# Cross attention block of a hybrid decoder step: order of the first loads and scores

## The chip, the cores and the metric

The kernel runs on 1 core of one Trainium2 chip. The metric is the device time of one execution in microseconds, as the median of several runs. The engines are called PE (TensorE), DVE (VectorE), ACT (ScalarE), POOL (GpSimd) and SP (SyncE, which issues DMAs).

## The reference, cut to what matters

The reference is one inference step of two trunk layers over two groups, a prompt of 1024 rows and a sample group of 8 sequences with 4 rows each. Each layer has a mixer and then a gated cross attention into 256 memory tokens with 4 heads of width 256. The prompt attends to keys and values made in the step, each sample sequence to its own cached keys and values:

```python
def cross_attn(h, mk, mv, w_qg, w_o):
    b, t, _ = h.shape
    q, g = jnp.split(h @ w_qg, 2, axis=-1)
    q = q.reshape(b, t, X_HEADS, X_HEAD_DIM)
    s = jnp.einsum('bthd,bmhd->bhtm', q, mk).astype(F32) * (X_HEAD_DIM ** -0.5)
    p = jax.nn.softmax(s, axis=-1).astype(h.dtype)
    o = jnp.einsum('bhtm,bmhd->bthd', p, mv).reshape(b, t, D_MODEL)
    return (o * jax.nn.silu(g)) @ w_o
```

## The kernel before, in words

In each of the two layers `cross_attention` (L2376) makes the prompt's keys KM and values VM, projects queries QT and gates SGX, runs `cross_both` (L2124), and then the output projection. Each of these parts is a block of its own: its instructions start when the block before is left, except that an engine with nothing more to do there is early and waits. The change is in `cross_both` alone.

`cross_both` has eight rounds and a ninth to drain. Round i works on tile i of the prompt (128 rows) and on sample sequence i. For the prompt, `scores` (L2184) makes the scores of a head in PSUM tile xS, `maximum` (L2275) reduces all four heads, `exponent` (L2338) exponentiates a head, `normalise` (L2281, L2283) scales, `turn` (L2197) and `turned` (L2348) transpose the probabilities, `values` (L2208) and `outputs` (L2289) make the result. For the sample, the cached keys of a sequence (1 MB, 128 partitions with two memory rows of 4 KB each) are loaded into one of two slots KB (L2156); `sample_keys` (L2220) turns a quarter of them, which is one head, with four transposes into the one PSUM tile zT; `sample_keys_out` (L2293) copies it to SBUF, and the next quarter may be turned only then. `sample_scores` (L2231) wants all four quarters. `sample_maximum` (L2299), `sample_exponent` (L2356) and `sample_normalise` (L2305, L2306) follow; the last multiplies with a column of the owner table xown, which is 1 where a row of the 32 belongs to the sequence. `sample_turn` (L2238), `sample_turned` (L2362) and `sample_values` (L2246) end the sequence, the last with the cached values (1 MB, two slots VB, L2175).

The order of work on each engine is written out by hand, engines meet by semaphores. A score call of one head shows as four matmul instructions in the trace, and four transposes make a quarter. In every round TensorE does `scores` and `sample_keys` of one head after the other, four times, then `turn` of the tile before, `sample_scores`, `values` and `sample_values` of the round before, `sample_turn`. VectorE does the four copies, then `maximum` and `sample_maximum`. SyncE asks for the keys of sequences 0 and 1 at once, then for the owner table (L2158) and for the gain vector gb of the output norm (L2159, read by the output projection), and for the keys of a later sequence once the slot's keys are turned (semaphore z_tp); after them come the output weights WO (L2163, L2166). GpSimd asks for the values of sequences 0 and 1 at once, and for later ones once the slot's value product is done (z_pv). VectorE waits for the owner table (z_m) before its first instruction in the block.

Of the kernel before, what the change touches and what calls it, by code (L numbers as in the profile page):

```python
# [22 lines left out]
P = 128  # L23
# [3 lines left out]
NB, TS = 8, 4  # L27
SMP = NB * TS
TOK = TP + SMP
NQ = TP // P  # L30
# [11 lines left out]
XH, XD = 4, 256  # L42
# [86 lines left out]
def build(nc, A, O):  # L129
# [4 lines left out]
    def sem(name):  # L134
        return top.enter_context(nc.semaphore(name))
# [1825 lines left out]
    def memory_keys_values(l, KM, VM, rows=(), gain=None, HT=None):  # L1961
# [153 lines left out]

    x_sc, x_nm, x_ex, x_pn, x_tp, x_te, x_pv, x_oe = (sem(n) for n in (
        "x_scores", "x_negmax", "x_exp", "x_normed", "x_probs_tp", "x_probs_out", "x_pv", "x_pv_out"))
    z_l, z_lv = [sem(f"memk_slot{k}") for k in range(2)], [sem(f"memv_slot{k}") for k in range(2)]
    z_m, z_tp, z_te, z_sc, z_nm, z_ex, z_pn, z_pt, z_pe, z_pv, z_oe = (sem(n) for n in (
        "z_mask", "z_k_tp", "z_k_out", "z_scores", "z_negmax", "z_exp", "z_normed", "z_probs_tp", "z_probs_out", "z_pv",  # L2120
# [3 lines left out]
    def cross_both(l, room, KM, VM, QT, SGX, WO, gb):  # L2124
# [5 lines left out]
        n0 = NQ * l  # L2130
        with ExitStack() as c:
# [17 lines left out]
            @block.sync  # L2149
            def _(sp):  # L2150
                w = A["x_w_o"][l].rearrange("(k p) n -> p k n", p=P)
                for b in range(NB):
                    if b >= 2:

                        sp.wait_ge(z_tp, 4 * (n0 + b - 1))
                    sp.dma_start(KB[b % 2], ck[:, b]).then_inc(z_l[b % 2], 16)  # L2156
                    if b == 1:
                        sp.dma_start(own[:], A["c_batch4"]).then_inc(z_m, 16)  # L2158
                        sp.dma_start(gb[:], A["norm_post_x"][l].partition_broadcast(P)).then_inc(y_g, 16)  # L2159

                for a in range(2):
                    sp.wait_ge(z_tp, 4 * (n0 + NB - 1 + a))
                    sp.dma_start(WO[:, 2 * a:2 * a + 2, :], w[:, 2 * a:2 * a + 2, :]).then_inc(y_w, 16)  # L2163
                for a in range(2):
                    sp.wait_ge(z_pv, n0 + NB - 1 + a)
                    sp.dma_start(WO[:, 4 + 2 * a:6 + 2 * a, :], w[:, 4 + 2 * a:6 + 2 * a, :]).then_inc(y_w2, 16)  # L2166
                sp.wait_ge(v_vout, 16 * (l + 1))

            @block.gpsimd
            def _(pool):  # L2170
                for b in range(NB):
                    if b >= 2:

                        pool.wait_ge(z_pv, n0 + b - 1)
                    pool.dma_start(VB[b % 2], cv[:, b]).then_inc(z_lv[b % 2], 16)  # L2175

            @block.tensor
            def _(pe):
                def scores(i, h):
                    if h == 0 and i:  # L2180

                        pe.wait_ge(x_ex, n0 + i)
                    for k in range(2):
                        m = nc.tensor.matmul(S[:, h * MEM:(h + 1) * MEM], QT[:, 2 * h + k, i * P:(i + 1) * P],  # L2184
                                             KM[:, 2 * h + k, :], start=k == 0, stop=k == 1)
                    if h == XH - 1:
                        m.then_inc(x_sc, 1)

                def turn(i):
                    pe.wait_ge(x_pn, n0 + i + 1)  # L2190
                    for a in range(2):
                        if i:

                            pe.wait_ge(x_te, 2 * (n0 + i - 1) + a + 1)
                        for h in (2 * a, 2 * a + 1):
                            for k in range(2):
                                t = nc.tensor.transpose(TPp[a][:, (2 * (h % 2) + k) * P:(2 * (h % 2) + k + 1) * P],  # L2197
                                                        PB[i % 2][:, h, k * P:(k + 1) * P], ident[:])
                        t.then_inc(x_tp, 1)

                def values(i, a):
                    pe.wait_ge(x_te, 2 * (n0 + i) + a + 1)
                    if 2 * i + a:

                        pe.wait_ge(x_oe, 2 * (n0 + i) + a)
                    for d in range(4 * a, 4 * a + 4):
                        for k in range(2):
                            m = nc.tensor.matmul(OV[:, d % 4 * P:(d % 4 + 1) * P], VM[:, k, d * P:(d + 1) * P],  # L2208
                                                 PT[i % 2][:, d // 2 * 2 + k, :], start=k == 0, stop=k == 1)
                    m.then_inc(x_pv, 1)  # L2210

                def sample_keys(b, q):
                    if q == 0:
                        pe.wait_ge(z_l[b % 2], 16 * (NB // 2 * l + b // 2 + 1))
                    if 4 * b + q:

                        pe.wait_ge(z_te, 4 * (n0 + b) + q)
                    for k in range(2):
                        for n in range(2):
                            t = nc.tensor.transpose(KTp[:, (2 * k + n) * P:(2 * k + n + 1) * P],  # L2220
                                                    KB[b % 2][:, n, (2 * q + k) * P:(2 * q + k + 1) * P], ident[:])
                    t.then_inc(z_tp, 1)

                def sample_scores(b):
                    pe.wait_ge(z_te, 4 * (n0 + b + 1))
                    if b:

                        pe.wait_ge(z_pe, n0 + b)
                    for k in range(2):
                        for h in range(XH):  # L2230
                            m = nc.tensor.matmul(SS[32 * h:32 * h + 32, 0:MEM], QT[:, 2 * h + k, TP:TOK], KBT[b % 2][:, 2 * h + k, :],  # L2231
                                                 start=k == 0, stop=k == 1, tile_position=(0, 32 * h))
                    m.then_inc(z_sc, 1)

                def sample_turn(b):
                    pe.wait_ge(z_pn, n0 + b + 1)
                    for k in range(2):
                        t = nc.tensor.transpose(SS[:, MEM + k * P:MEM + (k + 1) * P], PZ[b % 2][:, k * P:(k + 1) * P], ident[:])  # L2238
                    t.then_inc(z_pt, 1)

                def sample_values(b):
                    pe.wait_ge(z_pe, n0 + b + 1)
                    pe.wait_ge(z_lv[b % 2], 16 * (NB // 2 * l + b // 2 + 1))
                    for k in range(2):
                        for h in range(XH):
                            m = nc.tensor.matmul(OS[32 * h:32 * h + 32, 0:XD], PZT[b % 2][:, k, 32 * h:32 * h + 32],  # L2246
                                                 VB[b % 2][:, k, h * XD:(h + 1) * XD], start=b == 0 and k == 0,
                                                 stop=b == NB - 1 and k == 1, tile_position=(0, 32 * h), skip_group_check=True)
                    m.then_inc(z_pv, 1)

                for i in range(NQ + 1):
                    for h in range(XH):
                        if i < NQ:
                            scores(i, h)
                            sample_keys(i, h)
                    if i:
                        turn(i - 1)
                    if i < NQ:
                        sample_scores(i)
                    if i:  # L2260
                        values(i - 1, 0)
                        sample_values(i - 1)
                        values(i - 1, 1)
                    if i < NQ:
                        sample_turn(i)
                pe.wait_ge(z_oe, 3 * l + 1)
                for k in range(2):
                    t = nc.tensor.transpose(SS[:, k * P:(k + 1) * P], OZ[:, k * P:(k + 1) * P], ident[:])
                t.then_inc(z_pt, 1)

            @block.vector
            def _(dve):
                def maximum(i):
                    dve.wait_ge(x_sc, n0 + i + 1)
                    nc.vector.tensor_reduce(nm[:, i % 2, :], S[:].rearrange("p (h m) -> p h m", h=XH), AX.X, ALU.max, negate=True)\  # L2275
                        .then_inc(x_nm, 1)
# [28 lines left out]
                    dve_own.step(dve, nc.vector.reciprocal(zi[:, v], zsum[:, v]))  # L2305
                    nc.vector.tensor_scalar(PZ[b % 2][:], PZ[b % 2][:], zi[:, v], own[:, b:b + 1], ALU.mult, ALU.mult).then_inc(z_pn, 1)  # L2306

                dve.wait_ge(z_m, 16 * (l + 1))
                for i in range(NQ + 1):
                    if i < NQ:  # L2310
                        for q in range(4):
                            sample_keys_out(i, q)
                        maximum(i)
                        sample_maximum(i)
                    if i:
                        outputs(i - 1, 0)
                    if i < NQ:
                        sample_normalise(i)
                        normalise(i)
                    if i:  # L2320
                        outputs(i - 1, 1)
# [1020 lines left out]
```

## Time and profile before

| | us |
|---|---|
| median of 3 runs | 3042.34 |
| lowest and highest run | 3032.16, 3043.95 |
| the profiled execution, whole | 3035.24 |
| its span in the profile | 3033.5 |
| TensorE busy in it | 2711.2 |

The span runs from the first to the last instruction of the profiled execution; the execution's own time is 1.7 us longer. In the timeline a row gives the start, the duration, the engine, the line of the kernel and the names; a number in brackets is the idle time of that engine before the row, and what ended it. WO is the tile in which the slots KB and VB lie, HT the one with the turned keys and probabilities.

### The profile page before, as it was taken

Reading aid. Unit: us, or ns where it says so; the run is one execution under the profiler, and the core shown is the slowest. Engines: PE = TensorE matmul, PEld = TensorE weight load, DVE = VectorE, ACT = ScalarE, POOL = GpSimd, SP = SyncE. Lnnn points to the kernel's source line nnn. Section 1 sums busy time; section 2 is a strip of 40 time slices with the busy share of each in tenths; the row PEclk is TensorE's granted clock in tenths of the full one; section 3 lists DMA queues with packets and bytes.
Section 4 is the critical chain, followed back from the end, with each engine's and each line's share of the span. In section 5 each row is a group of like instructions: output and inputs, shape, how many; then the busy total and the mean of one; then the engine's idle time right before and its main releaser. Section 6 shows DMA issues by size and latency. Waiting matters only on the chain. (4 is left out here: it accounts for less than half of the span.)

```text
span 3033.5 us, 40100 instructions
## 1 busy us (share of the span) xinstructions
PE 2711.2 (89%) x16263; PEld 2170.5 (72%) x16263; DVE 1453.6 (48%) x2550; ACT 777.8 (26%) x1466; POOL 520.9 (17%) x419
## 2 busy tenths in 40 slices
PE   5999899998978998997999689776999996899898
PEld 4999566676766996686999467654555555699677
DVE  4998666564421004534665431156777673200453
ACT  3221355232312212322322112122121212221231
POOL 1012000341311210131212000012212221121012
PEclk9999899997989998997999799897998998999999
DMA  3211010862032114302322222284423203211531
GB/s 99 65 35 48 21 36 18 304 238 88 1 95 85 43 42 160 125 1 54 99 84 77 90 70 74 75 302 127 125 62 106 81 16 111 83 43 42 175 119 49
DMA packets 237754, 270.75 MB, mean 89 GB/s; under 512 B 36566, under 2 KB 190742, under 8 KB 232355
## 3 DMA queue, kind: packets, MB, share of 16 engines
q1 hardware_dynamic: 217762, 179.85, 20.0%
q0 software_dynamic: 16384, 75.77, 6.9%
q10 hardware_dynamic: 3456, 12.98, 1.0%
q8 instruction: 112, 1.84, 0.3%
q14 instruction: 40, 0.33, 0.0%
HBM read 226.66 MB, written 41.28 MB: 88 GB/s over the span
## 5 line engine op out<-in xcount | busy, mean ns | idle before, releaser
L297 PE MATMUL pp<-HH,WS_part 128*128 128x352 f32 x1776 | 574.2, 323 | 0.0
L295 PE MATMUL pp<-HH,WH 128*128 128x352 f32 x1344 | 436.3, 325 | 34.9 <-POOL WS_part L434 34.9
L296 PE MATMUL pp<-HT_part,WH 128*128 128x352 f32 x1344 | 434.5, 323 | 0.0
L297 PEld LDWEIGHTS pp<-HH,WS_part 128*128 128x128 f32 x1776 | 336.7, 190 | 0.0
L295 PEld LDWEIGHTS pp<-HH,WH 128*128 128x128 f32 x1344 | 254.2, 189 | 38.1 <-POOL WS_part L434 38.1
L296 PEld LDWEIGHTS pp<-HT_part,WH 128*128 128x128 f32 x1344 | 254.4, 189 | 0.0
L2293 DVE COPY HT<-zT 128x512 f32<-128x512 f32 x64 | 44.3, 692 | 437.0 <-DMA xown<-c_batch 383.8
L434 POOL TENSOR_TENSOR WS_part<-WS,WH 128x1024 fp32r<-128x1024 f32 x56 | 142.6, 2547 | 603.2 <-ACT WH L385 603.2
L2873 PE MATMUL OP<-oWO,YT 128*128 128x512 f32 x512 | 223.0, 593 | 1.3 <-DVE XE L3014 0.6
L2873 PEld LDWEIGHTS OP<-oWO,YT 128*128 128x128 f32 x512 | 96.5, 190 | 120.6 <-issue 119.8
L1048 DVE SCALAR_TENSOR_TENSOR CV<-GXP,cw,CV 128x512 f32<-128x512 f32 x240 | 161.9, 740 | 0.0
L295 PE MATMUL pp<-HH,CK_part 128*128 128x352 f32 x432 | 141.9, 328 | 7.9 <-DVE HT_part L913 7.9
L296 PE MATMUL pp<-HT_part,CK_part 128*128 128x352 f32 x432 | 140.4, 325 | 0.0
L295 PE MATMUL zp<-WZH,HH 128*128 128x512 f32 x256 | 103.9, 406 | 15.6 <-ACT ZS L2705 11.0
L2853 POOL TENSOR_TENSOR XK<-XK,Db 128x2048 f32<-128x2048 f32 (+1 forms) x9 | 88.1, 9788 | 141.9 <-DVE XD L3040 141.9
L295 PE MATMUL yp<-QT_part,KM_part 128*128 128x512 f32 x256 | 102.2, 399 | 2.3 <-DVE WO_part L628 2.3
L2509 DVE SCALAR_TENSOR_TENSOR oACC<-EP,cwo,oACC 128x1024 f32<-128x1024 f32 x72 | 98.7, 1370 | 9.2 <-DVE oACC L2507 2.4
L297 PE MATMUL zp<-WZH,HT_part 128*128 128x512 f32 x256 | 102.4, 400 | 0.0
L296 PE MATMUL zp<-WZ_part,HH 128*128 128x512 f32 x256 | 102.2, 399 | 0.0
L297 PE MATMUL yp<-QT_part,SGX_part 128*128 128x512 f32 x256 | 101.9, 398 | 0.0
L296 PE MATMUL yp<-WO_part,KM_part 128*128 128x512 f32 x256 | 101.7, 397 | 0.0
L2917 PEld LDWEIGHTS U<-XD,CBt 128*128 128x128 f32 (+1 forms) x576 | 78.6, 220 | 21.2 <-issue 16.4
(519 smaller groups left out, 5172.8 us busy)
## 6 DMA issues: line engine op xcount, KB each, us to landing
WS<-x_w_qg SPq DMA_DIRECT2D x32, 512.0 KB, 4.1
WO<-cache_mem_k SPq DMA_DIRECT2D x16, 1024.0 KB, 5.0
WO<-cache_mem_v POOLq DMA_DIRECT2D x16, 1024.0 KB, 5.6
CBt<-cum_scratch SPq DMA_DIRECT2D x8, 2048.0 KB
xbc_scratch<-oACC ACTq DMA_DIRECT2D x24, 528.0 KB, 2.7
WS<-o_w_in SPq DMA_DIRECT2D x24, 512.0 KB, 3.9
XT<-xbc_scratch SPq DMA_DIRECT2D x8, 1536.0 KB, 7.8
WS<-e_w_in SPq DMA_DIRECT2D x18, 512.0 KB, 3.9
```

Of the source, the lines that this page charges most:

```text
L295: nc.tensor.matmul(out, wh, xh, start=start, stop=False)
L296: nc.tensor.matmul(out, wh, xl, start=False, stop=False)
L297: return nc.tensor.matmul(out, wl, xh, start=False, stop=stop)
L434: nc.gpsimd.tensor_tensor(WL[:, k % slots, :, :], WS[:, k % slots, :, :], WH[k % 2][:, :, :], ALU.subtract).then_inc(p_lo, 1)
L1048: ins = nc.vector.scalar_tensor_tensor(out=out, in0=src, scalar=tap, in1=out, op0=ALU.mult, op1=ALU.add)
L2293: nc.vector.tensor_copy(KBT[b % 2][:, 2 * q:2 * q + 2, :], KTp[:].rearrange("p (k m) -> p k m", k=2))\
L2509: ins = nc.vector.scalar_tensor_tensor(out=out, in0=src, scalar=tap, in1=out, op0=ALU.mult, op1=ALU.add)
L2853: nc.gpsimd.tensor_tensor(XK[R, :].rearrange("p (h e) -> p h e", h=SH), XK[R, :].rearrange("p (h e) -> p h e", h=SH), Db[R, :].unsqueeze(2 ...
L2873: m = nc.tensor.matmul(OP[hf][0:T, :], YT[:, k, 0:T], WO[:, k, hf * 512:(hf + 1) * 512], start=k == 0, stop=k == NX - 1)
L2917: m = nc.tensor.matmul(U[g % 2][R, e * SP_:(e + 1) * SP_], CB[R, h, R], XD[R, h * SP_:(h + 1) * SP_], start=True, stop=True)
```

## The change

The first sequence's keys are requested in four column quarters, each with a semaphore z_q of its own, and each quarter's turning waits for its own semaphore. The owner table is requested directly behind the quarters, the keys of sequence 1 behind it, and gb behind the last key request. In round 0 TensorE makes the scores of all four heads of tile 0 before it turns a key; VectorE takes their maximum first, then copies, and waits for the owner table just before the first sample maximum. GpSimd requests the values of sequence 0 when two quarters of its keys are turned, those of sequence 1 when all four are. The waits on the two key slots are counted anew, since sequence 0 no longer signals them. Nothing in the arithmetic changes.

```diff
--- before.py
+++ after.py
@@ -2115,6 +2115,7 @@
 
     x_sc, x_nm, x_ex, x_pn, x_tp, x_te, x_pv, x_oe = (sem(n) for n in (
         "x_scores", "x_negmax", "x_exp", "x_normed", "x_probs_tp", "x_probs_out", "x_pv", "x_pv_out"))
+    z_q = [sem(f"memk_first{q}") for q in range(4)]
     z_l, z_lv = [sem(f"memk_slot{k}") for k in range(2)], [sem(f"memv_slot{k}") for k in range(2)]
     z_m, z_tp, z_te, z_sc, z_nm, z_ex, z_pn, z_pt, z_pe, z_pv, z_oe = (sem(n) for n in (
         "z_mask", "z_k_tp", "z_k_out", "z_scores", "z_negmax", "z_exp", "z_normed", "z_probs_tp", "z_probs_out", "z_pv",
@@ -2149,14 +2150,16 @@
             @block.sync
             def _(sp):
                 w = A["x_w_o"][l].rearrange("(k p) n -> p k n", p=P)
-                for b in range(NB):
+                for q in range(4):
+                    cols = slice(2 * q * P, (2 * q + 2) * P)
+                    sp.dma_start(KB[0][:, :, cols], ck[:, 0, :, cols]).then_inc(z_q[q], 16)
+                sp.dma_start(own[:], A["c_batch4"]).then_inc(z_m, 16)
+                for b in range(1, NB):
                     if b >= 2:
 
                         sp.wait_ge(z_tp, 4 * (n0 + b - 1))
                     sp.dma_start(KB[b % 2], ck[:, b]).then_inc(z_l[b % 2], 16)
-                    if b == 1:
-                        sp.dma_start(own[:], A["c_batch4"]).then_inc(z_m, 16)
-                        sp.dma_start(gb[:], A["norm_post_x"][l].partition_broadcast(P)).then_inc(y_g, 16)
+                sp.dma_start(gb[:], A["norm_post_x"][l].partition_broadcast(P)).then_inc(y_g, 16)
 
                 for a in range(2):
                     sp.wait_ge(z_tp, 4 * (n0 + NB - 1 + a))
@@ -2169,8 +2172,9 @@
             @block.gpsimd
             def _(pool):
                 for b in range(NB):
-                    if b >= 2:
-
+                    if b < 2:
+                        pool.wait_ge(z_tp, 4 * n0 + 2 * b + 2)
+                    else:
                         pool.wait_ge(z_pv, n0 + b - 1)
                     pool.dma_start(VB[b % 2], cv[:, b]).then_inc(z_lv[b % 2], 16)
 
@@ -2210,8 +2214,12 @@
                     m.then_inc(x_pv, 1)
 
                 def sample_keys(b, q):
-                    if q == 0:
-                        pe.wait_ge(z_l[b % 2], 16 * (NB // 2 * l + b // 2 + 1))
+                    if b == 0:
+                        pe.wait_ge(z_q[q], 16 * (l + 1))
+                    elif q == 0 and b % 2 == 0:
+                        pe.wait_ge(z_l[0], 16 * ((NB // 2 - 1) * l + b // 2))
+                    elif q == 0:
+                        pe.wait_ge(z_l[1], 16 * (NB // 2 * l + b // 2 + 1))
                     if 4 * b + q:
 
                         pe.wait_ge(z_te, 4 * (n0 + b) + q)
@@ -2249,9 +2257,13 @@
                     m.then_inc(z_pv, 1)
 
                 for i in range(NQ + 1):
+                    if i == 0:
+                        for h in range(XH):
+                            scores(0, h)
                     for h in range(XH):
+                        if 0 < i < NQ:
+                            scores(i, h)
                         if i < NQ:
-                            scores(i, h)
                             sample_keys(i, h)
                     if i:
                         turn(i - 1)
@@ -2305,12 +2317,15 @@
                     dve_own.step(dve, nc.vector.reciprocal(zi[:, v], zsum[:, v]))
                     nc.vector.tensor_scalar(PZ[b % 2][:], PZ[b % 2][:], zi[:, v], own[:, b:b + 1], ALU.mult, ALU.mult).then_inc(z_pn, 1)
 
-                dve.wait_ge(z_m, 16 * (l + 1))
+                maximum(0)
                 for i in range(NQ + 1):
                     if i < NQ:
                         for q in range(4):
                             sample_keys_out(i, q)
-                        maximum(i)
+                        if i:
+                            maximum(i)
+                        else:
+                            dve.wait_ge(z_m, 16 * (l + 1))
                         sample_maximum(i)
                     if i:
                         outputs(i - 1, 0)
```

## Rows read from the trace of the kernel before

**Rows 1.** The page: span and busy time of each engine (us, share, instructions).

```profile
span 3033.5 us, 40100 instructions
PE 2711.2 (89%) x16263; PEld 2170.5 (72%) x16263; DVE 1453.6 (48%) x2550; ACT 777.8 (26%) x1466; POOL 520.9 (17%) x419
```

**Rows 2.** Source line 2293: what its engine waited for (us, times), both layers.

```profile
  DMA xown<-c_batch: 383.8, 2
```

**Rows 3.** Timeline, layer 0: start, duration, engine, line, names [idle before, releaser].

```profile
1143.53 0.88 SPq L2156 DMA_DIRECT2D WO<-cache_mem_k  x2
...
1143.58 1.10 PE L2184 MATMUL xS<-KM,QT 128*128 128x256 f32 x4 [0.81 <-PEq L2392]
...
1150.28 1.12 PE L2220 MATMUL zT<-ident,WO 128*128 128x128 f32 x4 [5.59 <-DMA WO<-cache_mem_k]
...
1156.73 0.69 DVE L2293 COPY HT<-zT 128x512 f32<-128x512 f32 x1 [193.43 <-DMA xown<-c_batch]
...
1158.63 0.69 DVE L2293 COPY HT<-zT 128x512 f32<-128x512 f32 x1 [1.21 <-PE zT L2220]
...
1164.20 1.07 PE L2231 MATMUL zS<-HT,QT 128*32 128x256 f32 x16 [0.78 <-DVE HT L2293]
...
1166.23 0.47 ACT L2356 ACTIVATE PZ<-zS,znm 128x256 f32<-128x256 f32 x1
...
1167.49 0.69 PE L2238 MATMUL zS<-ident,PZ 128*128 128x128 f32 x2 [2.22 <-DVE PZ L2306]
...
1181.37 0.72 POOL L2175 DMA_DIRECT2D WO<-cache_mem_v  x1 [35.79 <-PE zO L2246]
1194.05 0.71 POOL L2175 DMA_DIRECT2D WO<-cache_mem_v  x1 [11.96 <-PE zO L2246]
```

**Rows 4.** Timeline, layer 1, the same events.

```profile
2809.65 1.10 PE L2184 MATMUL xS<-KM,QT 128*128 128x256 f32 x4 [0.81 <-PEq L2392]
...
2814.75 0.89 PE L2220 MATMUL zT<-ident,WO 128*128 128x128 f32 x4 [3.99 <-DMA WO<-cache_mem_k]
...
2827.13 1.07 PE L2231 MATMUL zS<-HT,QT 128*32 128x256 f32 x16 [0.78 <-DVE HT L2293]
...
2830.42 0.44 PE L2238 MATMUL zS<-ident,PZ 128*128 128x128 f32 x2 [2.22 <-DVE PZ L2306]
...
2841.76 0.71 POOL L2175 DMA_DIRECT2D WO<-cache_mem_v  x1 [29.82 <-PE zO L2246]
```

**Rows 5.** Timeline, layer 1: maximum of the scores, then a key step of sequence 1.

```profile
2826.99 1.22 DVE L2275 TENSOR_REDUCE xnm<-xS 128x4 f32<-128x1024 f32 x1
...
2833.03 0.66 PE L2220 MATMUL zT<-ident,WO 128*128 128x128 f32 x4
...
2833.53 1.03 PE L2184 MATMUL xS<-KM,QT 128*128 128x256 f32 x4
2833.73 0.69 DVE L2293 COPY HT<-zT 128x512 f32<-128x512 f32 x1 [0.75 <-PE zT L2220]
2834.47 0.66 PE L2220 MATMUL zT<-ident,WO 128*128 128x128 f32 x4
```

**Rows 6.** Time to landing: table (L2158), keys (L2156), values (L2175), a 256 KB load.

```profile
DMA to landing us min/median/max: 9.7/11.0/12.2
...
DMA to landing us min/median/max: 4.8/5.0/11.4
...
DMA to landing us min/median/max: 5.2/5.6/14.4
...
WV<-e_w_uv SPq DMA_DIRECT2D x1, 256.0 KB, 2.7
```

**Rows 7.** Windows: us, busy (instructions) of each engine, granted clock, DMA share, GB/s.

```profile
1145.00:1150.30 5.30, 0.02 (x1) 0.03 (x1) 0.00 (x0) 0.00 (x0) 0.58 (x1) 0.59 0.95 374
...
1163.50:1167.50 4.00, 1.08 (x17) 0.43 (x17) 2.78 (x5) 2.19 (x10) 0.00 (x0) 0.86 0.70 255
...
2825.30:2830.40 5.10, 2.12 (x23) 1.11 (x21) 2.95 (x6) 2.16 (x9) 0.00 (x0) 1.00 0.54 183
```

## The prediction

> **What bounds the kernel now.** The page comes first: TensorE is busy for 2711.2 of 3033.5 us [rows 1], so time is to be had only where it stands still or runs at the lower of its clock levels (1.2 instead of 2.4 GHz). The question is whether the change touches such a place. The view of one source line shows that the copies of turned keys out of PSUM (L2293) waited 383.8 us for the owner table [rows 2]. Nearly all of that is VectorE idling beside the projection, which costs nothing; the timeline tells what part is real. In layer 0 the block begins at 1143.58 with one head of scores. TensorE then stands 5.59 us until the first sequence's keys have landed, turns a quarter of them, and the first copy starts only at 1156.73, when the owner table is there, though the table is not read until much later. TensorE's next turning starts behind that copy. In layer 1 the same happens, with 3.99 us in the first gap [rows 3, 4]. These two openings are all that the change can shorten. Behind them the block is paced by TensorE: the value loads, each released by the value product of a sequence, are issued 12.68 us apart (1181.37 to 1194.05) [rows 3].
>
> I measure one layer from the start of its first scores to the issue of the third value load on GpSimd, which marks the end of the first sequence's value product: 1181.37 - 1143.58 = 37.8 us in layer 0, and 2841.76 - 2809.65 = 32.1 us in layer 1, together 69.9 us [rows 3, 4]. All that follows in the block, the loads of the output weights included, hangs on these events and shifts with them.
>
> **The change part by part**, in times from the start of the first scores.
>
> Scores in front. Four heads run back to back instead of one; a head takes 1.03 us at the high clock [rows 5], so TensorE has work until 4.0. No work is added, it is taken out of the gaps between the key steps. A key step is set by turning, copying and their handover, 1.44 us from one turning to the next with scores between them (2833.03 to 2834.47) [rows 5]; without the scores it stays at that.
>
> Key quarters. SyncE issues four requests in place of one, at 0.44 us each (0.88 us for two) [rows 3], so the first goes out at 0 and the last at 1.3. The first quarter (256 KB) has no row of its own kind. The bounds are 2.7 us, the landing of a 256 KB load of weights, and 5.0 us, the median landing of a whole 1 MB key load [rows 6]. I take 3.5, nearer to the row of the same size: the value loads no longer share the DMA engines. It is hidden by the 4.0 us of scores. At the upper end the first turning would start 1.0 late, of which the maximum below hides about half: 0.5 us per layer. A gain below zero is excluded, since TensorE has no place for the quarter before 4.0. The last quarter at its upper end is at 1.3 + 5.0 = 6.3, and is wanted at 8.4: nothing.
>
> Maximum in front of the copies. On VectorE the reduction of the first tile's scores takes 1.22 us [rows 5] and now starts at 4.05. The first quarter is turned at 4.7, the copy behind the reduction starts at 5.3: 0.6 us, in the sum. The copies then start at 5.3, 6.7, 8.2 and 9.6, and the sample scores follow 0.75 later, at 10.4. Before, they started at 20.6 (1164.20) and 17.5 (2827.13) [rows 3, 4].
>
> Sample softmax. From the sample scores to the turning of their probabilities it took 3.29 us (1164.20 to 1167.49) [rows 3]. The sample's exponential started at 1166.23, behind two exponentials of the prompt tile on ScalarE [rows 3]. These now run during the key steps, their maximum being ready at 5.3; I take off 0.4, nearly one exponential of 0.47 us. Turning is at 10.4 + 2.9 = 13.3.
>
> Owner table. It is waited for only before the sample maximum, at 11.4. Its request is fifth on SyncE's queue, at 1.8. Its landing took 9.7 to 12.2 us behind four loads of 1 MB [rows 6]; with 1 MB ahead of it I take the 5.0 of such a load, so 6.8. At the upper end it is there at 14.0 and costs 2.6 us per layer.
>
> Second keys. Requested at about 2.2, wanted at about 14; 5.0 to 11.4 us to landing [rows 6] gives 7.2 to 13.6. Hidden.
>
> Values. GpSimd now waits for the second quarter's turning (about 7) before it asks for the first values, and for the fourth's (about 10) before the second. With 5.2 to 14.4 us to landing [rows 6] the first are there by 21.4 at worst, and wanted about 1.4 before the end of the stretch, at 23 or later. Hidden. Nothing else is queued behind this wait on GpSimd in this block, and the second are wanted a whole round later.
>
> Gain vector of the output norm. Its request moves on SyncE behind the waits of six key loads, to about 75 us into the block. It is read only in the output projection, another 40 us on; a load of twice its size lands in 5.0. Free. The three added semaphore waits on TensorE are met whenever the key step is paced by the copy: nothing.
>
> **The clock sets the sum.** From the turning of the first sample's probabilities to the end of the stretch it took 11.34 us in layer 1 (2830.42 to 2841.76), where the clock stayed high, and 13.88 us in layer 0 (1167.49 to 1181.37), where it began low [rows 3, 4]. A key step at the low clock, without scores, is 1.90 us (copies at 1156.73 and 1158.63) [rows 3] against 1.44. From 4.0 to 13.3 TensorE now works 4 x 0.66 + 1.07 = 3.7 of 9.3 us, a share of 40% [rows 3, 5]. Two shorter stretches of before stand on both sides: 1.08 of 4.00 us, and the clock fell (mean 0.86); 2.12 of 5.10 us, and it held at 1.00 [rows 7]. Over 9 us at such a share I expect one fall in each layer, late in the key steps, with the high level back within the second round.
> So each layer: 13.3 + 0.5 (last key step) + 13.9 = 27.7 us. Two layers 55.4, against 69.9: **14.5 us less**. The profiled execution took 3035.24 us as a whole, 1.7 over its span; the sum makes it 3020.7. The median of the three runs shown is 3042.34, 7.1 higher, and I carry the gain over to it: 3027.8 us.
>
> The Trainium skill's "TensorE: Matmul & The Clock Gate", Part 4 (PE-mode transpose), says that transposes do not count as work for the clock. By that rule the key steps would look like idleness, and the fall would come earlier, which is the second rival.
>
> **The rivals.**
> 1. The clock holds. In both layers: 13.3 + 11.3 = 24.6 each, 20.7 us less, 3021.6. For it: layer 1 held the high level over 2.12 of 5.10 us. In one layer only: 24.6 + 27.7 = 52.3, 17.6 less, 3024.7. Chances 0.15 and 0.25.
> 2. The clock falls at the first key step in both layers. Four steps at +0.46, sample scores up to doubled (+1.07): 13.3 + 2.9 + 13.9 = 30.1 each, 9.7 less, 3032.6. For it: the gap of layer 0 had a mean of 0.59 directly after the first scores [rows 7]. Against: there TensorE did nothing at all. Chance 0.15. The rule of the page named above would make this the usual case; no row here has turnings alone, so I give it no more.
> 3. The transfers are the bound: quarters and owner table at their upper ends, 0.5 + 2.6 per layer, 6.2 off the forecast: 8.3 less, 3034.0. This is also how the change would fail to do what it says, the wait for the table only moving. For it: four small requests instead of one. Against: 3 MB less in front of the table. Chance 0.08.
> 4. Slower: the first values come too late, because they are asked for at 7 instead of at once, behind VectorE's copies and two key loads. They are wanted at about 26, so it decides from a landing of 19 us on. To undo 14.5 us it takes 7.3 more per layer, a landing of 26 us; at 36 us each layer loses 17, and the time is 3027.8 + 34 = 3062, 0.6% over before. The longest row is 14.4 us, with 4 MB under way [rows 6]. Chance 0.05.
> The Trainium skill's "SBUF — State Buffer" (the box on VectorE blocking DMAs) says that a GpSimd-issued load can wait while VectorE copies. In this trace value loads issued in mid-block beside a busy VectorE have the median of 5.6 us [rows 6], so the trace does not bear it out here.
>
> **How the numbers follow.** The forecast has 0.32, and is the likeliest single case. A measurement of this kernel can tell about 0.5% from no change, 15.2 us. Over that lie rival 1 almost whole (0.36) and about a third of the forecast, which is only 0.7 us short of it: 0.48. Slower by over 0.5%: a part of rival 4 and of drifts elsewhere, since the clock's dips in the rest of the kernel can fall otherwise: 0.04. The remaining 0.48 is within. The range goes from rival 1 to rival 3 with some 4 to 8 us for the spread of runs (3032 to 3044 before): 3013 to 3037.
>
> **What would show it.** Right: no idle time of VectorE put down to the owner table beyond the projection's; TensorE without a gap between first scores and first turning, or under 1 us; sample scores at about 10.4 to 11 in both layers; the third value load issued at 24.6 to 30; the granted clock dipping between 6 and 20. Wrong: a wait of TensorE on key quarters of over 1 us; the sample maximum waiting for the table; a wait of the value product on its load; a round other than 12.68 us behind the stretch.

## The result, and the profile after

| | before | changed |
|---|---|---|
| median of 8 runs, us | 3041.07 | 3023.76 |
| lowest and highest run | 3032.16, 3048.75 | 3013.81, 3029.82 |
| span of the profiled execution | 3033.5 | 3027.9 |
| stretch in layer 0, first scores to third value load | 37.8 | 27.8 |
| stretch in layer 1 | 32.1 | 27.7 |

The changed kernel is 17.3 us faster by the medians, a ratio of 0.9947 with a 95% interval of 0.9929 to 0.9966, which is 10 to 22 us. The forecast was 3027.8 us, which is 14.5 us less than the median of three runs it started from. The two stretches were to become 27.7 us each and are 27.79 and 27.73, together 14.4 less than before.

The timeline of the changed kernel, layer 0, answers to [rows 3]. Columns are start, duration, engine, line, names and, in brackets, idle time before the row and its releaser. Scores are L2188, turning L2228, copies L2305, sample scores L2239, sample turning L2246, value loads L2179.

```profile
1144.02 1.91 SPq L2155 DMA_DIRECT2D WO<-cache_mem_k  x4
...
1144.08 3.69 PE L2188 MATMUL xS<-KM,QT 128*128 128x256 f32 x16 [0.81 <-PEq L2407]
...
1147.61 0.60 PE L2228 MATMUL zT<-ident,WO 128*128 128x128 f32 x4
1147.81 1.22 DVE L2287 TENSOR_REDUCE xnm<-xS 128x4 f32<-128x1024 f32 x1 [183.88 <-PE xS L2188]
1148.95 0.68 DVE L2305 COPY HT<-zT 128x512 f32<-128x512 f32 x1
...
1150.44 0.69 DVE L2305 COPY HT<-zT 128x512 f32<-128x512 f32 x1 [0.81 <-PE zT L2228]
...
1153.45 0.69 DVE L2305 COPY HT<-zT 128x512 f32<-128x512 f32 x1 [0.81 <-PE zT L2228]
...
1154.20 1.94 PE L2239 MATMUL zS<-HT,QT 128*32 128x256 f32 x16 [0.79 <-DVE HT L2305]
...
1158.01 0.69 PE L2246 MATMUL zS<-ident,PZ 128*128 128x128 f32 x2 [1.87 <-DVE PZ L2318]
...
1171.87 0.71 POOL L2179 DMA_DIRECT2D WO<-cache_mem_v  x1 [17.40 <-PE zO L2254]
```

The same in layer 1, for [rows 4].

```profile
2810.08 3.69 PE L2188 MATMUL xS<-KM,QT 128*128 128x256 f32 x16 [0.81 <-PEq L2407]
...
2820.38 1.94 PE L2239 MATMUL zS<-HT,QT 128*32 128x256 f32 x16 [0.78 <-DVE HT L2305]
...
2824.18 0.69 PE L2246 MATMUL zS<-ident,PZ 128*128 128x128 f32 x2 [1.87 <-DVE PZ L2318]
...
2837.81 0.71 POOL L2179 DMA_DIRECT2D WO<-cache_mem_v  x1 [17.18 <-PE zO L2254]
```

The reader is to see three things. TensorE goes from its sixteen score matmuls into the first turning without a gap, and VectorE's bracket names the scores, no longer the owner table. The copies follow each other at 1.50 us. And the sample scores take 1.94 us instead of 1.07: the clock has fallen just before. Windows of the changed kernel say the same (us, busy of PE, PEld, DVE, ACT, POOL, granted clock, DMA share, GB/s): first the microsecond of the last turning and the one after it in layer 0, then both layers from the first turning to the sample turning.

```profile
1153.00:1154.00 1.00, 0.42 (x4) 0.18 (x2) 0.55 (x1) 0.00 (x0) 0.27 (x1) 0.70 0.85 336
1154.00:1155.00 1.00, 0.80 (x8) 0.40 (x12) 0.14 (x1) 0.00 (x0) 0.46 (x1) 0.50 1.01 401
...
1147.60:1158.00 10.40, 4.43 (x33) 2.22 (x31) 4.90 (x8) 2.28 (x9) 1.52 (x2) 0.78 0.94 301
2813.60:2824.20 10.60, 4.63 (x34) 2.26 (x32) 4.90 (x8) 2.30 (x10) 1.51 (x2) 0.76 0.87 290
```

Landing times of the changed kernel answer to [rows 6]: owner table, key quarters, values.

```profile
DMA to landing us min/median/max: 3.7/4.2/4.7
...
DMA to landing us min/median/max: 2.7/3.6/5.1
...
DMA to landing us min/median/max: 5.2/5.7/9.8
```

**Where the spans differ.** The profiled spans are only 5.6 us apart, though the stretches gave 14.4. The rest is in code that the change does not touch. From the first state load of layer 1's mixer to the store of its state it took 2529.08 - 1962.31 = 566.8 us before and 2529.34 - 1952.98 = 576.4 us after. First the kernel before, then the changed one:

```profile
1962.31 49.13 SPq L3179 DMA_DIRECT2D fSB<-state_ssm  x8
...
2529.08 0.38 SPq L3148 DMA_DIRECT2D out<-SNat  x1
```

```profile
1952.98 52.27 SPq L3194 DMA_DIRECT2D fSB<-state_ssm  x8
...
2529.34 0.38 SPq L3163 DMA_DIRECT2D out<-SNat  x1
```

In the ten kernels profiled below this part took 562.9 to 573.2 us, in no order that follows the edits; the changed kernel's is the longest of all twelve. Whether the edit has a part in that is not shown; that its median over eight runs is 17.3 us lower speaks against a loss in every run. One span cannot show a gain of 14 us here; the stretches, which are measured inside the block, can. They are what the experiments are compared by, beside the medians. Each is read from one profiled execution; where two kernels should be alike there (changed and table late), their stretches agree to 0.1 us.

### The profile page after: what moved, and what is told of

Its sections match the earlier page's. It is cut to its first block and busy times, and to the rows that moved or that the text cites. A ratio compares the mean times of both kernels' runs of the same rounds, so it can differ in the third digit from the quotient of the medians.

```text
span 3027.9 us, 40112 instructions
## 1 busy us (share of the span) xinstructions
PE 2714.4 (90%) x16263; PEld 2173.4 (72%) x16263; DVE 1453.7 (48%) x2550; ACT 777.4 (26%) x1466; POOL 519.6 (17%) x419
## 5 line engine op out<-in xcount | busy, mean ns | idle before, releaser
L2287 DVE TENSOR_REDUCE xnm<-xS 128x4 f32<-128x1024 f32 x16 | 19.4, 1216 | 367.6 <-PE xS L2188 367.6
## 6 DMA issues: line engine op xcount, KB each, us to landing
CBt<-cum_scratch SPq DMA_DIRECT2D x8, 2048.0 KB, 10.3
```

## The experiments

Each stretch is counted from the first scores to the issue of the third value load, as in the prediction. A ratio compares the runs of a kernel with runs of the kernel before that were made beside them; behind it stands its 95% interval.

| run | sample scores at | stretch, layers 0 and 1 | sum | ratio to before |
|---|---|---|---|---|
| before | 20.6, 17.5 | 37.8, 32.1 | 69.9 | |
| changed | 10.1, 10.3 | 27.8, 27.7 | 55.5 | 0.9947 (0.9929 to 0.9966) |
| order only | 20.7, 18.4 | 38.2, 35.1 | 73.3 | 1.0006 (0.9991 to 1.0022) |
| loads only | 10.0, 9.9 | 25.9, 27.1 | 53.0 | 0.9948 (0.9928 to 0.9968) |
| wait only | 15.2, 12.6 | 31.3, 28.6 | 60.0 | 0.9970 (0.9954 to 0.9985) |
| busy clock | 10.1, 10.1 | 24.4, 24.4 | 48.8 | 0.9916 (0.9895 to 0.9938) |
| values at once | 15.4, 15.1 | 32.0, 31.7 | 63.8 | 0.9978 (0.9963 to 0.9993) |
| whole load | 11.3, 11.5 | 28.4, 28.2 | 56.7 | 0.9954 (0.9938 to 0.9970) |
| loads and busy clock | 8.7, 9.0 | 23.3, 23.6 | 46.9 | 0.9934 (0.9919 to 0.9950) |
| table late | 10.1, 10.3 | 27.8, 27.7 | 55.5 | 0.9957 (0.9939 to 0.9975) |
| whole, values at once | 11.5, 11.7 | 28.3, 28.5 | 56.8 | 0.9954 (0.9931 to 0.9977) |
| two heads first | 8.8, 9.0 | 25.2, 25.4 | 50.6 | 0.9944 (0.9924 to 0.9965) |

### Which part gives the gain

**Wait only**, to the kernel before:

```diff
-                dve.wait_ge(z_m, 16 * (l + 1))
                 for i in range(NQ + 1):
...
                         maximum(i)
+                        if i == 0:
+                            dve.wait_ge(z_m, 16 * (l + 1))
```

> The kernel before with one thing changed: VectorE waits for the owner table just before the first sample maximum instead of at the start of the block. Theory A (two late arrivals lie in series with work behind them, keys and table): the first turning stays at 6.7 and 5.1 us, the copy follows at once, sample scores at 12 to 15 and 11 to 14 us, the table is there by then or 1 us late; stretches about 31 to 33 and 27 to 30 us, 7 to 12 us less in sum than before, two thirds of the change's gain. Rival B (the table is only a symptom, the load queue is the bound): under 4 us less in sum.

Timeline of this run, layer 0:

```profile
1140.82 1.10 PE L2184 MATMUL xS<-KM,QT 128*128 128x256 f32 x4 [0.81 <-PEq L2393]
...
1147.61 1.12 PE L2220 MATMUL zT<-ident,WO 128*128 128x128 f32 x4 [5.69 <-DMA WO<-cache_mem_k]
...
1148.76 0.69 DVE L2293 COPY HT<-zT 128x512 f32<-128x512 f32 x1 [188.08 <-PE zT L2220]
...
1155.98 1.07 PE L2231 MATMUL zS<-HT,QT 128*32 128x256 f32 x16 [0.78 <-DVE HT L2293]
...
1172.15 0.72 POOL L2175 DMA_DIRECT2D WO<-cache_mem_v  x1 [29.34 <-PE zO L2246]
```

The first turning is as late as before, 6.79 us after the scores, but the copy follows 1.15 behind it instead of 6.45. The sum is 9.9 less, inside the 7 to 12 of theory A, and 69% of the change's 14.4. The ratio says 9.1 us (5 to 14). One moved wait gives two thirds of it. The copies and sample scores came where theory A had them but for 15.2 us in layer 0, 0.2 beyond its range.

**Order only**, to the kernel before: the new order of scores and maximum, everything else old.

```diff
+                    if i == 0:
+                        for h in range(XH):
+                            scores(0, h)
                     for h in range(XH):
-                        if i < NQ:
+                        if 0 < i < NQ:
                             scores(i, h)
+                        if i < NQ:
                             sample_keys(i, h)
...
                 dve.wait_ge(z_m, 16 * (l + 1))
+                maximum(0)
```

> The kernel before with only the order changed: scores of tile 0 and their maximum in front of the key steps; loads, owner table and its wait as before. Stretch = from the first scores to the issue of the third value load (before 37.8 and 32.1 us in layers 0 and 1, changed kernel 27.8 and 27.7). Theory A (the loads and the wait for the owner table set the opening, the order alone gives little): copies still start at about 13 and 11 us, only the key steps get shorter (1.5 to 1.9 us instead of 1.9 to 2.6); stretches 34 to 37 and 29 to 32 us, 1 to 6 us less in sum. Rival B (the order gives the gain, by filling TensorE): about the 27.8 of the changed kernel in both, 14 less in sum.

Timeline of this run, layer 1:

```profile
2821.01 1.23 DVE L2279 TENSOR_REDUCE xnm<-xS 128x4 f32<-128x1024 f32 x1 [190.68 <-DMA xown<-c_batch]
2822.15 0.68 DVE L2297 COPY HT<-zT 128x512 f32<-128x512 f32 x1
...
2822.89 1.11 PE L2220 MATMUL zT<-ident,WO 128*128 128x128 f32 x4 [7.13 <-DVE HT L2297]
...
2828.58 1.94 PE L2231 MATMUL zS<-HT,QT 128*32 128x256 f32 x16 [0.78 <-DVE HT L2297]
```

Theory A was right that the copies still start late (14.3 and 11.9 us) and had the sum wrong: instead of 1 to 6 us less it is 3.4 more. The maximum now stands behind the table's wait and in front of the first copy, and with the scores gone from the key steps these run at the low clock, sample scores included (1.94 us). The median does not move. The order alone is no gain; rival B falls.

**Loads only**, to the changed kernel: its loads and waits, the old order of round 0.

```diff
-                    if i == 0:
-                        for h in range(XH):
-                            scores(0, h)
                     for h in range(XH):
-                        if 0 < i < NQ:
+                        if i < NQ:
                             scores(i, h)
-                        if i < NQ:
                             sample_keys(i, h)
...
-                maximum(0)
```

> The changed kernel with the old order of round 0 (one head of scores, one quarter of keys, in turn; maximum behind the copies); quarters, early owner table, late wait for it and late value requests stay. Theory A (the first quarter lands at about 3.5 us, before four heads of scores are done): the first turning starts at about 3.5 instead of 3.6 us, no maximum is in front of the first copy, and the scores lie in the shadow of the copies, so TensorE is busier: sample scores at 9 to 9.7 us, stretches 24 to 27 us, 1 to 3 us less than in the changed kernel in each layer. Rival B (the scores in front are needed to hide the first quarter): first turning at 4.5 us or later, stretches 28 us or more.

First turning at 2.69 and 2.76 us, sample scores 0.1 and 0.4 earlier than in the changed kernel, sum 2.5 less. By the ratio the two are the same. So beside the quarters the scores in front bring nothing; in the profiled executions they cost 1.9 and 0.6 us in the two openings, which the ratios do not show. What held theory A back from 9.0 is the first key step, which TensorE enters after 1.59 us of waiting and takes 2.4 us for.

### The two loads that meet

**Whole load**, to the changed kernel:

```diff
-                for q in range(4):
-                    cols = slice(2 * q * P, (2 * q + 2) * P)
-                    sp.dma_start(KB[0][:, :, cols], ck[:, 0, :, cols]).then_inc(z_q[q], 16)
+                sp.dma_start(KB[0], ck[:, 0]).then_inc(z_q[0], 16)
...
-                        pe.wait_ge(z_q[q], 16 * (l + 1))
+                        pe.wait_ge(z_q[0], 16 * (l + 1))
```

> The changed kernel, but the first sequence's keys come in one request of 1 MB in place of four quarters. Theory A (the quarters only pull the first turning from the landing of the whole to the end of the scores): without the value loads beside it the whole lands at 4.8 to 5.2 us, first turning then instead of 3.53, copies 0.9 to 1.1 us later since the maximum hides the rest, stretches 28.4 to 29.2 us. Rival B (the whole lands as late as before, 5.1 and 6.7 us, or the quarters' 1 KB runs cost as much as they bring): stretches of 30 us and more in the first case, unchanged at 27.8 in the second.

The whole load lands in 4.9 to 5.0 us, the stretches are 0.5 to 0.6 longer than with quarters. The four quarters are worth 1.1 us in sum. The lower ends of the expected range were met or passed by 0.2.

**Values at once**, to the changed kernel:

```diff
-                    if b < 2:
-                        pool.wait_ge(z_tp, 4 * n0 + 2 * b + 2)
-                    else:
+                    if b >= 2:
                         pool.wait_ge(z_pv, n0 + b - 1)
```

> The changed kernel, but GpSimd requests the values of sequences 0 and 1 at the start of the block, as before. Theory A (they share the DMA engines with the key quarters and the table): the quarters land later, the last at 6 to 9 us, the table at 8 to 11 us; stretches 28.5 to 31 us against 27.8 and 27.7. Rival B (the quarters are in front and small enough, the deferral is not needed): stretches within 0.3 us of the changed kernel's for the same clock, 27.5 to 28.1 us.

TensorE in layer 0 of this run, and the landing of its quarters:

```profile
1149.49 0.63 PE L2226 MATMUL zT<-ident,WO 128*128 128x128 f32 x4 [1.57 <-DVE HT L2303]
1154.02 1.12 PE L2226 MATMUL zT<-ident,WO 128*128 128x128 f32 x4 [3.89 <-DMA WO<-cache_mem_k]
1157.27 1.11 PE L2226 MATMUL zT<-ident,WO 128*128 128x128 f32 x4 [2.13 <-DMA WO<-cache_mem_k]
```

```profile
DMA to landing us min/median/max: 2.7/6.8/12.0
```

The effect of theory A, larger than it said: two quarters are waited for, the slowest of the eight lands after 12.0 us, the table after 10.9 and 11.7, and the sum is 8.2 over the changed kernel's. The kernel before had the same values beside a whole key load, which was there after 6.7 us in layer 0 and 5.1 in layer 1. The next run asks why.

**Whole, values at once**: both edits together.

> The whole-load run with the value loads requested at once as well: the same 1 MB of keys beside the same values as in the values-at-once run, but in runs of 4 KB instead of 1 KB. Theory A (in the values-at-once run the queue with small packets got the small share of the engines beside the value loads' larger ones, which is why the last quarters came at 12 us and more): with 4 KB runs the keys land as in the kernel before, at 5.1 to 6.8 us, and the stretches are 28.5 to 30.5 us, shorter than the 32.0 and 31.7 of the quarters. Rival B (it is only the bytes: 1 MB more beside the keys costs the same in either shape): keys at 9 us or later, stretches of 31.5 us or more.

The whole load lands in 5.1 to 5.3 us beside the values, and the sum is 56.8, the same as with deferred values (56.7). Theory A holds, with one stretch 0.2 below its range. So it is not the two megabytes of values by themselves that hurt but their meeting with keys in small pieces. The DMA queues of the two runs in layer 0, whose blocks start within 0.2 us of each other, show two reasons (queue: packets, MB, share of 16 engines; q1 is SyncE's, q0 GpSimd's). First from 1143 to 1148 us, quarters and then whole:

```profile
q1 hardware_dynamic: 548, 0.53, 32.6%
q0 software_dynamic: 20, 0.08, 26.5%
```

```profile
q1 hardware_dynamic: 236, 0.97, 56.2%
```

The whole load has moved nearly all of its megabyte before the values move anything; the quarters have moved half of theirs when the values begin. Then from 1151 to 1153 us, in the same order:

```profile
q0 software_dynamic: 170, 0.66, 80.4%
q1 hardware_dynamic: 174, 0.17, 23.8%
```

```profile
q1 hardware_dynamic: 102, 0.42, 52.0%
q0 software_dynamic: 102, 0.40, 50.2%
```

In both runs the two queues move equally many packets, but a packet of the quarters holds 1 KB and one of the values or of a whole load 4 KB: 0.17 MB of keys beside 0.66 MB of values, against 0.42 beside 0.40. The Trainium skill's "DMA: Bandwidth & Descriptors" (Queues, rings and completion order) says that an engine takes its queues in turn, packet by packet. The equal counts agree with that, though a packet of that page can hold several of the packets that the profile counts. No run parts the two reasons, and neither explains that from 1147 to 1148 us both queues of the first run together moved only 0.06 MB, against 0.43 MB in the second.

Beside no values the quarters are not free either: in the first 7 us of the block in layer 0 SyncE's queue moved 1.57 MB in the changed kernel and 2.10 MB in the whole-load run. There the pieces were in time all the same.

This run also says where the rest of the gain lies. Its stretches, 28.3 and 28.5 us, stand 3.0 and 0.2 below the wait-only run's, without quarters and without deferred values; those two together give only another 1.3 us, of the 4.5 that the moved wait leaves. What it has over the wait-only run is the scores in front, the table's request ahead of the second keys', and gb's at the end. In layer 0 the first keys were there 5.1 us after the start instead of 6.8, and the key steps took 1.5 us, the last 2.0, instead of 2.6, 2.5 and 1.5. The keys are not earlier for the order of the scores (6.5 us in the order-only run). Beyond that no run separates these edits; the scores in front, of no use beside the quarters, may be of use beside a whole load.

**Table late**, to the changed kernel: the request for the owner table back behind the second keys, the late wait kept.

```diff
-                sp.dma_start(own[:], A["c_batch4"]).then_inc(z_m, 16)
                 for b in range(1, NB):
...
+                    if b == 1:
+                        sp.dma_start(own[:], A["c_batch4"]).then_inc(z_m, 16)
```

> The changed kernel with the owner table requested behind the second keys, as before; the late wait for it stays. Theory A (with the wait moved, the table's place in the queue does not matter, since it is wanted only at about 12 us): it lands 6 to 9 us after its request, before the sample maximum; stretches as in the changed kernel, 27.5 to 28.1. Rival B (the table lands as late as before, 12 to 14 us after the start): the sample maximum waits for it, stretches 28.5 to 30 us.

It lands 7.6 to 8.2 us after its request and nothing waits for it; the stretches are the changed kernel's to 0.1 us. The place of the request is worth nothing here once the wait is where the table is used.

### The clock

**Busy clock**, to the changed kernel:

```diff
+                def busy(n):
+                    for _ in range(n):
+                        for k in range(2):
+                            nc.tensor.matmul(TPp[1][:, 0:MEM], QT[:, k, 0:P], KM[:, k, :], start=k == 0, stop=k == 1)
...
                             sample_keys(i, h)
+                        if i == 0:
+                            busy(1)
...
                         sample_scores(i)
+                    if i == 0:
+                        busy(2)
```

> The changed kernel with extra matmuls in round 0 whose result is not used: two behind each quarter's turning, four behind the first sample scores, as long as the gaps that TensorE has there. Theory A (the falling clock costs about 3 us in each layer, 27.7 against 24.6): the granted clock stays high through the key steps and the first round; sample scores take 1.07 instead of 1.94 us, stretches 24.4 to 25.5 us, about 6 us less in sum than in the changed kernel. Rival B (the clock falls anyway, or the extra work is itself in the way): stretches of 27.5 us or more.

TensorE in layer 0 of this run with the third value load, and the window up to the sample turning:

```profile
1148.26 0.63 PE L2228 MATMUL zT<-ident,WO 128*128 128x128 f32 x4
1148.73 1.03 PE L2262 MATMUL xT<-KM,QT 128*128 128x256 f32 x4
...
1151.19 1.07 PE L2239 MATMUL zS<-HT,QT 128*32 128x256 f32 x16
1152.19 1.99 PE L2262 MATMUL xT<-KM,QT 128*128 128x256 f32 x8
1154.13 0.44 PE L2246 MATMUL zS<-ident,PZ 128*128 128x128 f32 x2
...
1165.47 0.71 POOL L2179 DMA_DIRECT2D WO<-cache_mem_v  x1 [14.03 <-PE zO L2254]
```

```profile
1144.60:1154.20 9.60, 8.88 (x58) 6.14 (x57) 4.89 (x8) 2.36 (x10) 1.52 (x2) 1.00 0.90 269
```

The key steps keep their 1.50 us, the clock stays at 1.00, the sample scores are back at 1.07 and the stretches are 24.41 and 24.40. That is 3.4 and 3.3 us per layer from work that computes nothing, and the price of the clock in the prediction (27.7 against 24.6, 3.1 us) measured by itself. The sum is 21.1 less than before; the ratio says 25.5 (19 to 32), which holds it.

**Loads and busy clock**, to the loads-only run:

```diff
                             scores(i, h)
+                            if i == h == 0:
+                                busy(1)
                             sample_keys(i, h)
+                    if i == 0:
+                        busy(1)
...
                         sample_scores(i)
+                    if i == 0:
+                        busy(2)
```

> The kernel of the loads-only run (old order of round 0, all load changes) with extra matmuls of unused result: two before the first quarter is waited for, two behind the last quarter's turning, four behind the first sample scores. Theory A (order and clock are separate terms: the old order loses nothing, its low clock does): first turning at 2.7, key steps 1.45 us, sample scores at 8.5 to 9 us, clock high, stretches 23 to 24 us, 1 us less than the busy-clock run in each layer. Rival B (the scores in front are what keeps the clock up, or later quarters are late): sample scores at 10 us or later, stretches of 24.4 us or more.

Order and clock are two terms: with the clock held, the old order is 0.8 to 1.1 us shorter per layer than the scores in front. The ratios do not show it: they point the other way (0.9934 against 0.9916), with intervals that overlap.

**Two heads first**, to the loads-only run, without extra work:

```diff
                     for h in range(XH):
                         if i < NQ:
-                            scores(i, h)
+                            if i:
+                                scores(i, h)
+                            else:
+                                for s in ((0, 1), (2,), (3,), ())[h]:
+                                    scores(0, s)
                             sample_keys(i, h)
```

> The loads-only run with another order of its own work and no extra matmuls: two heads of scores, then quarter, head, quarter, head, quarter, quarter. Theory A (the first gap of that run, 1.6 us of waiting for the quarter, made the clock low in its first key step): first turning at 2.7, key steps 1.45 us, sample scores at 8.5 to 9.2 us, then the clock falls in some layers; stretches 24.5 to 26.5 us. Rival B (nothing over the loads-only run, whose stretches were 25.9 and 27.1): sample scores at 9.9 us or later, or stretches of 26.5 us or more.

First turning at 2.68 and 3.01, in layer 0 after a wait of 0.72 us, key steps of 1.5 us from the first on, and the clock falls only with the sample scores (1.54 and 1.85 us). Of the orders tried that do no extra work it has the shortest stretches, 5.0 us under the changed kernel's in sum; the ratios cannot tell these two apart.

## Why the prediction was right

**Scores in front.** Said: until 4.0. Measured: 3.69, with the first turning at 3.53, the head's 1.03 us overlapping its neighbours. It was right that this is where the first turning starts and that the quarters are hidden: the fastest of the eight landed in 2.7 us, the slowest in 5.1. In the loads-only run, where TensorE waits for it, the first quarter let the turning start at 2.7; the 3.5 taken for it was too high, and cost the sum nothing because the scores hide it.

**Maximum and key steps.** Said: copies at 5.3, 6.7, 8.2, 9.6, sample scores at 10.4. Measured: 4.87, 6.36, 7.87, 9.37 and 10.12 in layer 0. The start is 0.4 earlier for the reason above, the step 1.50 instead of 1.44. The sample scores in both layers (10.1 and 10.3) were a little earlier than the 10.4 to 11 named as a sign of being right.

**Sample softmax.** Said: 2.9 from sample scores to turning, and 0.5 for a slow last key step. Measured: 3.81 and 3.80, and a last key step of 1.50 and 1.68. The sum of both terms is right (3.4 said, 3.8 measured, beside the 0.3 that the sample scores were early), but the placing is off: the clock fell with the last turning, and its price there was the sample scores, 0.87 us longer, which the forecast had only in its second rival. The two exponentials did go off the chain: before, the sample's exponential waited behind them, now it starts 0.04 us after its maximum. That early scores, a late turning and the last key step add up to the forecast within 0.1 us is in part luck.

**The clock.** Said: one fall in each layer in a stretch where TensorE works 40%, back within the second round. Measured: 4.43 of 10.40 us and 4.63 of 10.60 busy, a share of 43 and 44%, one fall in each, 13.86 and 13.63 us from the turning to the end against the 13.9 taken from layer 0 of before. That the clock would fall in both layers was a choice between two shorter stretches of before, one on each side, with a chance of 0.32; it was not derived. Rival 1, the clock that holds, is what the busy-clock run makes: 24.4 against its 24.6. The rule on transposes in the Trainium skill's "TensorE: Matmul & The Clock Gate", Part 4 (PE-mode transpose), was read as asking for an earlier fall, at the first key step; in the changed kernel it came with the last one, some 6 us after the last score matmul. In the order-only run the key steps behind the first were slow, but they stood behind gaps of 7.39 and 7.13 us. No run separates turnings from idle time beyond that, so the rule stays open.

**The loads.** Table, second keys and values were costed at nothing, and nothing waits for them. Rival 3 did not come: no quarter was waited for in the profiled execution. Rival 4 did not come: the values landed in 9.8 us at most. What the prediction did not say is that the deferred values are a condition of the quarters, not a side of them. It named the missing value loads as a reason for its 3.5 us and gave them no price; leaving them in costs 4.1 us per layer. Nor did it divide the gain: two thirds come from the wait, which it only counted among the other terms.

**The sum.** 14.5 said, 14.4 measured in the stretches, 17.3 in the medians with an interval of 10 to 22. The forecast lay just short of 0.5% and the ratio just beyond it (0.53%); the interval, 0.34 to 0.71%, holds both.

## What to carry to other kernels

Look for a wait that stands in front of a chain and not in front of the instruction that needs the data: moving it was two thirds of this gain. When a load is cut into small pieces so that work may start early, keep other queues' large packets away until the pieces are there, or leave it whole; here the whole load with nothing deferred was only 1.3 us behind the deferred quarters, in the sum of both openings. And where a chain alternates short TensorE work with another engine, the clock's fall is part of its price: TensorE work in the gaps, useful if there is any, took 3.3 to 3.4 us off each opening of some 28.

## What the runs showed of the hardware

Four requests of 256 KB, each in 1 KB runs, landed in 2.7 to 5.1 us in the changed kernel, in up to 6.1 us with the second keys directly behind them, and in up to 12.0 us beside two 1 MB loads of another queue. A single 1 MB request of 4 KB runs took 5.1 to 5.3 us beside the same loads; in layer 0 of the kernel before, with the second keys directly behind it, it was there after 6.7 us. Two queues with work for the same engines moved equally many packets (170 and 174, 102 and 102 in 2 us), whatever the packets held. Sixteen sample score matmuls took 1.07 us at the high clock and 1.94 at the low. In the changed kernel the granted clock fell from 1.00 to 0.50 behind the key turnings with copies between them; with unused matmuls in the same gaps it stayed at 1.00. The same mixer code took between 562.9 and 576.4 us in twelve profiled executions.
